# Two transformer blocks on one core: powers for the SSM tiles from coefficient tables, twelve broadcast products and sums a tile in place of a chain of five complex products

## The reference

```python
ab = exp((lr + i*li) * dt)                    # per group (64) and state (64)
bu = einsum('blgc,gpc->blgp', ug, f * b)      # f = (ab - 1) / (lr + i*li)
s  = associative_scan(ab, bu)                 # s[t] = ab * s[t-1] + bu[t]
y  = einsum('blgp,gcp->blgc', s, c) + d * ug  # real part
```

## Time and profile before

| | |
|---|---|
| median of 3 runs | 2621.66 us (2621.43 to 2622.06) |
| the profiled execution | 2616.89 us |
| its span | 2615.2 us |
| mean granted clock of TensorE | 0.976 |

### The profile page before, as it was taken

The page is one execution under the profiler, slowest core; times in us unless marked ns, Lnnn a source line. Parts: engine busy times, 40 slices in busy tenths (PEclk is TensorE's granted clock), DMA queues, the critical chain, the costliest instruction groups (busy, mean ns, idle before and its releaser), DMA issues.

```text
span 2615.2 us, 50525 instructions
## 1 busy us (share of the span) xinstructions
PE 2492.9 (95%) x18072; PEld 2361.3 (90%) x18072; DVE 1723.6 (66%) x2553; ACT 1195.8 (46%) x1791; POOL 662.3 (25%) x1071
## 2 busy tenths in 40 slices
PE   7999999989999998988988999999999999999999
PEld 7899999888899998988887999999988888888888
DVE  7876766567777767677777766565555555555555
ACT  5344444445555555544444434434444444444443
POOL 3300121358778884222112222011000000000000
PEclk9999999999999999999989999999999999999999
DMA  6655575555555554544445676675677777677774
GB/s 235 207 179 196 180 218 179 184 176 169 171 176 182 187 186 160 177 161 167 132 137 163 217 237 218 204 227 172 190 194 188 185 187 187 187 185 186 186 186 158
DMA packets 217450, 484.85 MB, mean 185 GB/s; under 512 B 22761, under 2 KB 120725, under 8 KB 217089
## 3 DMA queue, kind: packets, MB, share of 16 engines
q1 hardware_dynamic: 182912, 415.29, 52.3%
q0 software_dynamic: 13216, 37.93, 4.7%
q10 hardware_dynamic: 21216, 30.22, 3.5%
HBM read 455.00 MB, written 31.08 MB: 186 GB/s over the span
## 4 chain that ended last, share of the span: by engine, by line
PE 71%; DVE 12%; issue 10%; ACT 3%; POOL 3%; ACTq 1%; DVEq 0%; DMA 0%; POOLq 0%
PE z_ps L1988 13%; PE z_ps L1989 13%; PE z_ps L1990 13%; PE z_ps L2324 6%; PE z_ps L2325 6%; PE z_ps L2330 6%; DVE w_lo L1299 4%; ACT w_hi L723 2%; PE o_ps L2359 1%; PE o_ps L2358 1%; PE o_ps L2357 1%; PE v_ps L2358 1%; PE v_ps L2357 1%; PE p_ps L2358 1%; PE p_ps L2357 1%
## 5 line engine op out<-in xcount | busy, mean ns | idle before, releaser
L1299 DVE TENSOR_TENSOR w_lo<-w_raw,w_hi 128x1024 fp32r<-128x1024 f32 x520 | 644.4, 1267 | 333.0 <-ACT w_hi L723 331.2
L1988 PE MATMUL z_ps<-x_hi,w_hi 128*128 128x256 f32 x2816 | 825.0, 293 | 17.9 <-DVE w_lo L1292 14.1
L1989 PE MATMUL z_ps<-x_lo,w_hi 128*128 128x256 f32 x2816 | 807.7, 287 | 0.0
L1990 PE MATMUL z_ps<-x_hi,w_lo 128*128 128x256 f32 x2816 | 807.0, 287 | 0.0
L723 ACT ACTIVATE w_hi<-w_raw 128x1024 fp32r<-128x1024 f32 x520 | 533.1, 1052 | 256.9 <-PE z_ps L1990 208.9
L1988 PEld LDWEIGHTS z_ps<-x_hi,w_hi 128*128 128x128 f32 x2816 | 552.1, 196 | 30.0 <-issue 20.8
L1989 PEld LDWEIGHTS z_ps<-x_lo,w_hi 128*128 128x128 f32 x2816 | 551.9, 196 | 1.0
L1990 PEld LDWEIGHTS z_ps<-x_hi,w_lo 128*128 128x128 f32 x2816 | 551.3, 196 | 0.0
L1878 DVE TENSOR_TENSOR w_lo<-w_raw,w_hi 128x1024 fp32r<-128x1024 f32 x262 | 320.6, 1225 | 315.0 <-ACT w_hi L1143 314.9
L1143 ACT ACTIVATE w_hi<-w_raw 128x1024 fp32r<-128x1024 f32 x262 | 278.1, 1062 | 427.5 <-PE z_ps L2330 270.3
L2324 PE MATMUL z_ps<-w_hi,x_hi 128*128 128x512 f32 x704 | 275.1, 391 | 0.6 <-DVE res L1854 0.6
(11 more groups left out here) (383 smaller groups left out, 4192.7 us busy)
## 6 DMA issues: line engine op xcount, KB each, us to landing
w_raw<-in_w SPq DMA_DIRECT2D x704, 512.0 KB, 4.2
w_raw<-in_w SPq DMA_DIRECT2D x80, 384.0 KB, 4.9
res<-tab_d POOLq DMA_DIRECT2D x32, 384.0 KB, 4.6
w_raw<-in_w SPq DMA_DIRECT2D x80, 128.0 KB, 2.9
tab_d<-arena ACTq DMA_DIRECT2D x32, 256.0 KB, 2.1
tab_d<-arena POOLq DMA_DIRECT2D x32, 128.0 KB, 3.4
sg_d<-arena ACTq DMA_DIRECT2D x32, 128.0 KB, 4.4
arena<-sg_d POOLq DMA_DIRECT2D x16, 256.0 KB, 3.8
```

The costliest lines, as they stand in the source:

```text
L1299: dve.tensor_tensor(w_lo[:, n % RING, :], w_raw[:, n % RING, :], w_hi[:, n % RING, :].bitcast(F32), ALU.subtract).then_inc(w_lo_ready, 1)
L1988: pe.matmul(z, wh, hi[:, kt, :], start=(first and i == 0), stop=False)
L1989: pe.matmul(z, wh, lo[:, kt, :], start=False, stop=False)
L1990: m = pe.matmul(z, wl, hi[:, kt, :], start=False, stop=(last and i == len(kts) - 1))
```

## The change

Coefficient tables are made once on GpSimd (`coefficients`): `c_coef` holds f lam^m for m = 0 to 4, `b_coef` holds lam^m for m = 3 to 1, for all 32 tiles. A tile's powers are then products of C (5 x 32 elements a partition) and of B (3 x 32) with these, both operands broadcast: six instructions each, twelve steps. The temporaries of a tile are in `sq`. Therefore tile 0's powers are made behind all 16 squares of layer 0, no longer in their middle. The tables lie in the second half of `sq_sum` and in `t_vec`, which moves in the arena; `times_in` is copied out of `t_vec` to a packed tile of 64 elements, and VectorE reads that copy.

```diff
+        c_coef = arena[:, 6 * T:6 * T + 320].rearrange("p (r m s) -> p r m s", r=2, m=5)
+        b_coef = arena[:, 6 * T + 320:8 * T].rearrange("p (r m s) -> p r m s", r=2, m=3)
+        c_tmp = sq[:, 0:160].rearrange("p (m c) -> p m c", m=5)
+        b_tmp = sq[:, 160:256].rearrange("p (m c) -> p m c", m=3)
...
+        times_in = tile_mem[:, 1920:1920 + NC]
+        coef_t = tile_mem[:, 1984:2048].rearrange("p (r s) -> p r s", r=2)
...
-            XT_STEPS = 15
+            COEF_STEPS = 21
+            XT_STEPS = 12
+
+            def coefficients():
+
+                pool.tensor_scalar(times_in, t_vec.rearrange("p (k i) -> p k i", i=STEP)[:, :, 0], 1.0, None,
+                                   ALU.mult).then_inc(xt_step, 1)
+                pool.tensor_scalar(c_coef[:, :, 0, :], ssm_c[:, 0:2, :], 1.0, None, ALU.mult).then_inc(xt_step, 1)
+                pool.wait_ge(xt_step, 1)
+                pool.tensor_scalar(b_coef[:, :, 2, :], ssm_lam[:], 1.0, None, ALU.mult).then_inc(xt_step, 1)
+                pool.wait_ge(xt_step, 3)
+                at = 3
+                lam = [ssm_lam[:, r, :].unsqueeze(1).to_broadcast([P, 2, ST]) for r in range(2)]
+                powers = [(c_coef, m, m + 1) for m in range(4)] + [(b_coef, m, m - 1) for m in (2, 1)]
+                for table, m, to in powers:
+                    pool.tensor_tensor(coef_t, table[:, :, m, :], lam[1], ALU.mult).then_inc(xt_step, 1)
+                    pool.tensor_tensor(table[:, :, to, :], table[:, :, m, :], lam[0], ALU.mult).then_inc(xt_step, 1)
+                    pool.wait_ge(xt_step, at + 2)
+                    pool.tensor_tensor(table[:, 0, to, :], table[:, 0, to, :], coef_t[:, 1, :], ALU.subtract)
+                    pool.tensor_tensor(table[:, 1, to, :], table[:, 1, to, :], coef_t[:, 0, :], ALU.add).then_inc(xt_step, 1)
+                    at += 3
+                    pool.wait_ge(xt_step, at)
 
             def tile_powers(st):
...
-                times(x[:, :, 0, :], c_in, xt_t[:, :, 0, :], f_r, f_i, 0)
...
+                pool.tensor_tensor(c_tmp, c_im, by(c_coef, 1, 5), ALU.mult).then_inc(xt_step, 1)
+                pool.tensor_tensor(c_out[0], c_re, by(c_coef, 0, 5), ALU.mult).then_inc(xt_step, 1)
+                pool.tensor_tensor(c_out[1], c_im, by(c_coef, 0, 5), ALU.mult).then_inc(xt_step, 1)
+                pool.wait_ge(xt_step, at + 2)
+                pool.tensor_tensor(c_out[0], c_out[0], c_tmp, ALU.subtract).then_inc(xt_step, 1)
+                pool.wait_ge(bt_ready, st + 1)
+                pool.tensor_tensor(b_tmp, b_im, by(b_coef, 1, 3), ALU.mult).then_inc(xt_step, 1)
+                pool.wait_ge(xt_step, at + 4)
+                pool.tensor_tensor(c_tmp, c_re, by(c_coef, 1, 5), ALU.mult).then_inc(xt_step, 1)
+                pool.tensor_tensor(b_out[0], b_re, by(b_coef, 0, 3), ALU.mult).then_inc(xt_step, 1)
+                pool.wait_ge(xt_step, at + 6)
                 if st + 1 < ST:
                     load_c(st + 1)
-                pool.wait_ge(bt_ready, st + 1)
-                for m in range(3):
-                    times(x[:, :, m + 1:8 - m:6 - 2 * m, :], x[:, :, m:9 - m:8 - 2 * m, :], xt_t, l_r, l_i, 3 + 3 * m)
-                times(x[:, :, 4, :], x[:, :, 3, :], xt_t[:, :, 0, :], l_r, l_i, 12)
+                pool.tensor_tensor(c_out[1], c_out[1], c_tmp, ALU.add).then_inc(xt_step, 1)
+                pool.tensor_tensor(b_out[1], b_im, by(b_coef, 0, 3), ALU.mult).then_inc(xt_step, 1)
+                pool.wait_ge(xt_step, at + 7)
+                pool.tensor_tensor(b_out[0], b_out[0], b_tmp, ALU.subtract).then_inc(xt_step, 1)
+                pool.wait_ge(xt_step, at + 10)
+                pool.tensor_tensor(b_tmp, b_re, by(b_coef, 1, 3), ALU.mult).then_inc(xt_step, 1)
                 pool.dma_start(tab_d[st][:, 4 * P:TAB].rearrange("p (r b c) -> p r b c", r=2, b=4),
                                x[:, :, 1:5, :]).then_inc(f_stored[e], 16)
+                pool.wait_ge(xt_step, at + 11)
+                pool.tensor_tensor(b_out[1], b_out[1], b_tmp, ALU.add).then_inc(xt_step, 1)
...
+            pool.wait_ge(t_vec_landed, 16)
+            coefficients()
             load_c(0)
-            with pool.Fori(0, KT // 2) as n:
+            with pool.Fori(0, KT) as n:
                 sum_squares(0, n, False)
-            tile_powers(0)
-            with pool.Fori(KT // 2, KT) as n:
-                sum_squares(0, n, False)
-            for st in range(1, ST):
+            pool.wait_ge(sq_summed, summed(0, KT))
+            for st in range(ST):
                 tile_powers(st)
...
-            times_in = t_vec.rearrange("p (k i) -> p k i", i=STEP)[:, :, 0]
...
                     dve.wait_ge(consts_landed, (7 + STEP) * 16)
+                    dve.wait_ge(xt_step, 21)
...
-                if l == 0:
-                    dve.wait_ge(t_vec_landed, 16)
...
-                pe.wait_ge(xt_step, 15 * st + 15)
+                pe.wait_ge(xt_step, 21 + 12 * st + 12)
```

More of the change, by code:

```diff
@@ L126, in build @@
         top[1] = top[0]
-        rel_at = top[0]
+        t_vec = part(1, 1, row)
         cos_r, sin_r, rstd_m, msq = (part(1, 1, row) for _ in range(4))
-        rope_cos, rope_sin, sqf, msq_sum, t_vec = (part(1, 1, row) for _ in range(5))
+        rope_cos, rope_sin, sqf, msq_sum = (part(1, 1, row) for _ in range(4))
+        c_coef = arena[:, 6 * T:6 * T + 320].rearrange("p (r m s) -> p r m s", r=2, m=5)
+        b_coef = arena[:, 6 * T + 320:8 * T].rearrange("p (r m s) -> p r m s", r=2, m=3)
+        c_tmp = sq[:, 0:160].rearrange("p (m c) -> p m c", m=5)
+        b_tmp = sq[:, 160:256].rearrange("p (m c) -> p m c", m=3)
         tile_at = top[0]
@@ L567, in tile_powers, with over, by @@
-                times(x[:, :, 0, :], c_in, xt_t[:, :, 0, :], f_r, f_i, 0)
+                def over(v, n):
+                    return v.unsqueeze(1).to_broadcast([P, n, 32])
+                def by(table, r, n):
+                    return table[:, r, :, st].unsqueeze(2).to_broadcast([P, n, 32])
+                c_re, c_im, b_re, b_im = over(c_in[:, 0, :], 5), over(c_in[:, 1, :], 5), over(x[:, 0, 8, :], 3), over(x[:, 1, 8, :], 3)
+                c_out, b_out = [x[:, r, 0:5, :] for r in range(2)], [x[:, r, 5:8, :] for r in range(2)]
```

13 lines of the change are left out of this document (1 added, 12 removed).

## The result

The kernel after takes 2656.60 us (median of 4 runs, 2654.07 to 2659.22) against 2621.55 for the kernel before beside it: a ratio of 1.0142, 95% interval 1.0127 to 1.0157, or 33 to 41 us slower. The forecast was 2628.7 us, range 2622.5 to 2634. The sign is right, the size is not: the loss is some 35 us, and seven were forecast.

The account below looks back on a forecast made before the run. TensorE, busy for 95% of the span, was taken as the bound, with odd tiles waiting for VectorE. Stall 7.7 + clock 2.5 - packed times 3.2 = +7.0 us gave 2628.7 us, range 2622.5 to 2634.

Parts of the forecast that it names:

- Rival D: TensorE's 27.4 us of waits charged to GpSimd are really GpSimd's and vanish: 2602 us, faster; chance 0.03.
- Rivals B and E: B: short stall at tile 0, 2622.7 us, chance 0.17; E: broadcasts double GpSimd's arithmetic, 2634 us, chance 0.08.
- Step 1: GpSimd's powers per tile: 2 to 3 us saved, worth nothing in the steady state, covered by its 10 us lead.
- rival C: VectorE's angle and half-clock stretches behind odd tiles: shorter GpSimd work lets VectorE gain more, 2616 to 2623 us; chance 0.10.
- Step 2: Tile 0's powers, made behind all 16 sums, stall TensorE at tile 0: +7.7 us, bounds 4.5 and 9.
- Step 3: TensorE's clock falls to half after the new gap at tile 0: +2.5 us (0 to 2.8).
- Step 4: VectorE's angle reads packed times, 0.2 us less for each of 16 odd tiles' waits: -3.2 us (-1.6 to -4.5).
- Step 5: Making the coefficient tables on GpSimd, under 14 us, fits its idle time before the first square: costs nothing.

Follow-up runs that it names:

- e12_stt: Kernel after with the three TENSOR_SCALARs of VectorE's angle made SCALAR_TENSOR_TENSORs, GpSimd untouched: 2649.38 us, ratio 1.0123 to the kernel before.
- e1_early: Kernel after with tile 0's powers back in the middle of the sum over squares, temporaries elsewhere: 2649.28 us, ratio 1.0107 to the kernel before.
- e4_before_late: Kernel before with only tile 0's powers moved behind all 16 squares: 2631.03 us, ratio 1.0045.
- e3_before_packed: Kernel before with only the packed times, copied once by VectorE: 2616.27 us, ratio 0.9982.
- e15_before_tt: Kernel before with only the TENSOR_SCALARs of GpSimd's products made TENSOR_TENSORs with the coefficient's column broadcast: 2627.71 us, ratio 1.0036.
- e10_two_gates_last: Kernel after with early tile 0, GpSimd's odd-tile powers and even-tile B parts waiting for VectorE's preparation, both DMA issues last: 2625.73 us, ratio 1.0023.
- e9_two_gates: Kernel after with early tile 0, GpSimd's odd-tile powers and even-tile B parts waiting for VectorE's preparation: 2640.17 us, ratio 1.0071.
- e11_plain: Kernel after with plain operands of the same size in place of the broadcast ones in the powers' products: 2653.55 us, ratio 1.0128.

## Why the prediction was wrong, step by step

**Right: who ends the waits.** The 27.4 us charged to GpSimd did not fall when its work shrank, and the profile after names L1449. Rival D was worth its 3 in 100. Rivals B and E did not come either: the stall was 6.0 us long, and the broadcasts cost no more than plain operands.

**Step 1, "in the steady state the saved 2 to 3 us are worth nothing": the step that failed.** The arithmetic was near: 0.46 and 0.35 us undisturbed (medians of 0.54 and 0.37 from tile 1 to tile 31) where 0.52 and 0.37 were taken. GpSimd's lead did cover its own time: its store of an odd tile now ends 22 us before TensorE starts the tile, at the median, where it was 9. And yet this stretch, put at -3, came out at +21.9 us. What the step left out is that an engine off the path can still act on the one that is on it. I had priced the two engines' contention from VectorE to GpSimd (4.1 us at tile 0) and looked at the other direction only through `w_lo`, whose median does not move even now (1226 ns, maximum from 1354 to 1577). The median of a long instruction is the wrong probe: the sum of `w_lo` did grow, by 4.4 us, while a hold of a few tenths triples an instruction of 0.2 us. The short ones stood in the earlier trace rows, with 389 ns over 262, and I read that as something to gain, because GpSimd would be busy for less time. It is busy for less, but the time in which it is busy holds more.

The loss was then doubled by TensorE's clock: 10.9 us of waits and 10.9 us of slower matmuls. The half clock behind a wait was in the forecast for tile 0 and, with its sign turned, in rival C; that it would come behind 12 odd tiles in place of 6 was not.

For the exclusion that rival C weighed, the Trainium skill (SBUF — State Buffer, Who interferes with whom) says that a VectorE instruction with at most one SBUF input, outside the two-port modes, does not contend with GpSimd, that one with two SBUF inputs contends with a GpSimd instruction that reads SBUF, and that `tensor_scalar` is among the operations that can enter the two-port modes. The runs agree on two inputs: in the kernel before, from tile 1 to tile 31, GpSimd's L559 at 128 elements has a median of 1465 ns in the 20 cases beside `w_lo`, which has two, and of 603 in the 53 beside neither `w_lo` nor the angle. On one input they decide nothing, because the TENSOR_SCALARs of the angle may be in a two-port mode: one of 64 elements takes 195 ns at the least (L1442), one of 256 takes 283 (L1394), an estimated 0.46 ns for each further element, where `w_lo` takes 1.2 ns an element. The same step with one SBUF tensor (kernel after) and with two (e12_stt) is held alike, 502 and 500 ns at the median, 906 and 905 at most, which goes with the Trainium skill.

**Step 2, the stall at tile 0:** 7.7 us forecast, 6.0 measured (bounds 4.5 and 9), with the mechanism that was named. GpSimd ran from 552.16 to 561.54, which is 9.4 us where 11 to 11.7 were forecast (548.8 to 559.8 or 560.5), and its instructions beside the four `w_lo` took up to 1.36 us for 0.35:

```profile
556.44 1.32 POOL L603 TENSOR_TENSOR arena<-arena 128x96 f32<-128x96 f32 x1
557.73 1.36 POOL L605 TENSOR_TENSOR arena<-arena 128x96 f32<-128x96 f32 x1
559.17 1.21 POOL L607 TENSOR_TENSOR arena<-arena 128x96 f32<-128x96 f32 x1
560.33 0.80 POOL L608 DMA_DIRECT2D tab_d<-arena  x1
```

Undoing it (e1_early) gives back 7.3 us, or 9 by the ratios, about what stall and clock cost together (6.0 + 2.6).

**Step 3, the half clock behind it:** +2.5 us forecast, +3.4 from tile 0 to tile 1 in the kernel after, of which 0.6 is a longer wait at tile 1; +2.7 in e4_before_late.

**Step 4, the packed times:** -3.2 us forecast (16 tiles by 0.2), not borne out. Alone, in e3_before_packed, tiles 1 to 31 gain 2.4 us, and 3.2 lies within the interval of 0.3 to 8.9; but that nearness is luck as far as the record shows. The way by which it should have come, 16 waits shorter by 0.2 us, is absent (21.2 us of odd waits against 21.3), and the price was too high: the medians fell by 22 ns (L1399), nothing (L1400) and 43 ns (L1405), where 60, 70 and 70 were counted (line numbers of the kernel before). Most of the 102 ns between L1405 and L1402 is not the stride: packed, L1405's median is still 285 ns and L1402's 226. So the trace does not agree with the 93 ns that the forecast worked out from the Trainium skill (Vector Engine (DVE) Microarchitecture Reference, Measured stream behaviour on trn2): its 2.50 ns a column are for both sources, or the result, stepping at every element, and here one source steps. In the kernel after, what gain there is lies hidden under the holds.

**Step 5, the coefficients:** 426.61 to about 439.7 us, 13 us, and the first square still idles 16.70 us ahead. Nothing, as forecast.

**Rival C had the place right and the sign wrong.** It named L1399 behind GpSimd's instructions and the half-clock stretches behind odd tiles, and took fewer busy microseconds for less contention.

**Sum.** Forecast 7.7 + 2.5 - 3.2 = 7.0. Profiled: 6.0 + 3.4 + 21.9 + 2.2 (after tile 31) + 3.5 (scatter ahead of tile 0) = 37.0.

**What is open.** Why VectorE's angle is held more beside GpSimd's TENSOR_TENSORs (48.4 us in sum in e15_before_tt) than beside its TENSOR_SCALARs (41.9) is not shown: no run changed the kind and kept the durations. Nor does one show how the remaining 13 us share between the length of the new instructions and their lack of gaps; gates and late DMA issues together give 15 us back, so where GpSimd's work falls decides most of the loss, whatever its kind. e10_two_gates_last still takes 7.4 us more than before from tile 1 to tile 31. No form with the coefficient tables beat the kernel before.

## What to carry to other kernels

An engine with slack is not free: before making its work shorter by fewer, denser instructions, look at what the engine on the path does in the same microseconds. Its shortest instructions show a hold first (minimum, median, maximum). Then add up the durations of each of its lines, long ones too, because a median can stand still while the sum grows. Moving the dense work only moves the victim, so follow the whole chain ahead of a wait, not the last link. A wait that grows by half a microsecond may cost twice that where TensorE's clock falls behind it.

## What the hardware showed unexpectedly

- In e9_two_gates a VectorE instruction of 0.28 us took 1.55 us (1.54 at the median of 16), across the end of a DMA issue, a sum and two products of GpSimd and into a third: it waited for a run of instructions, not for one.
- Both engines hold each other, but not the same instructions. GpSimd is stretched beside the long `w_lo`, whatever its own kind: at 128 elements from 603 to 1465 ns as TENSOR_SCALAR (L559 before) and from 400 to 709 ns as TENSOR_TENSOR (L564 in e15_before_tt), medians from tile 1 to tile 31. Beside the angle it hardly is (642 and 413 ns), and there it is VectorE that takes longer.
- VectorE's instructions with one and with two SBUF tensors were held alike (502 and 500 ns for some 0.25 undisturbed).
- On GpSimd, broadcast operands cost no more than plain ones: medians of 541 and 538 ns for 160 elements, 373 and 389 for 96 (kernel after and e11_plain, tiles 1 to 31).
